# Which bank and which step two of a pair's projection thirds take, in a two-layer decoder step on one Trainium2 core

## The reference, cut to what matters

```python
q, z, gl, gate = b_project(xp, c_prompt, b_norm_g[j], b_w_ada[j], b_b_ada[j], b_w_in[j])
o_cmp, o_sel, o_win = nsa_prompt(q, comp_p[:, :, 0], comp_p[:, :, 1], gather_p, win_p, rel_bias_table)
...
ob = jnp.stack([o_cmp, o_sel, o_win], axis=2).reshape(n, t, N_BRANCH, N_HEADS, HEAD_DIM)
mix = jnp.sum(jax.nn.sigmoid(gl)[..., None] * ob * jax.nn.silu(z), axis=2)
```

## Time and profile before

| what | value |
|---|---|
| median of 3 runs | 1786.0 us (1785.25 to 1787.79) |
| the profiled execution | 1782.46 us, its span 1780.7 us |
| PE busy | 1623.2 us, 91% of the span |
| DVE, ACT, POOL busy | 911.3, 599.7, 501.1 us |
| mean granted clock of PE | 0.950 |

### The profile page before, as it was taken

One profiled execution on the slowest core, in us unless ns is written; L12 is line 12 of the kernel. 1 busy time (PEld: TensorE's weight loads), 2 busy tenths in 40 slices (PEclk: granted clock), 3 DMA queues, 4 the chain that ended last, 5 costly groups with the idle time before them and its releaser, 6 DMA issues.

```text
span 1780.7 us, 31773 instructions
## 1 busy us (share of the span) xinstructions
PE 1623.2 (91%) x11976; PEld 1453.3 (82%) x11976; DVE 911.3 (51%) x2356; ACT 599.7 (34%) x1315; POOL 501.1 (28%) x304
## 2 busy tenths in 40 slices
PE   3899999997896988799999999999999999998887
PEld 1688888886795987788888889888898888976777
DVE  1445455455325143455655556556555565577355
ACT  2523333343004042224434344343443434443112
POOL 0131322116531234281111111111102111049462
PEclk9899999999898988899999999999999999999998
DMA  9123232223321144310111131111110111133822
GB/s 351 50 99 125 92 111 101 101 102 132 119 95 72 54 165 126 86 36 22 39 37 34 31 77 40 60 34 28 34 40 13 34 28 34 28 98 110 270 72 107
DMA packets 81586, 146.20 MB, mean 82 GB/s; under 512 B 19059, under 2 KB 52883, under 8 KB 81267
## 3 DMA queue, kind: packets, MB, share of 16 engines
q1 hardware_dynamic: 68202, 129.69, 22.5%
q10 hardware_dynamic: 10288, 8.46, 1.5%
q0 software_dynamic: 2944, 6.04, 1.2%
HBM read 130.01 MB, written 19.35 MB: 84 GB/s over the span
## 4 chain that ended last, share of the span: by engine, by line
PE 81%; DVE 7%; ACT 4%; issue 3%; DMA 3%; SPq 1%; POOL 0%; ACTq 0%; DVEq 0%
PE PS L935 15%; PE PS L937 14%; PE PS L936 14%; PE PS L1182 9%; PE PS L1195 9%; PE PS L1162 4%; PE PS L1163 4%; PE PS L1274 2%; PE PS L1172 1%; PE PS L1191 1%; PE PS L1127 1%; PE PS L966 1%; ACT XT L1383 1%; ACT HT_r L1386 1%; DMA KD<-w_bo 1%
## 5 line engine op out<-in xcount | busy, mean ns | idle before, releaser
L935 PE MATMUL PS<-HT_r,WR_r 128*128 128x344 f32 x1368 | 461.7, 337 | 29.2 <-DVE XT_r L1650 24.4
L937 PE MATMUL PS<-HT_r,WR_r 128*128 128x344 f32 x1368 | 445.0, 325 | 0.0
L936 PE MATMUL PS<-XT_r,WR_r 128*128 128x344 f32 x1368 | 444.7, 325 | 0.0
L625 POOL TENSOR_TENSOR WR_r<-WR,ONE 128x1024 fp32r<-128x1024 f32 x65 | 125.8, 1936 | 1093.4 <-DMA WR<-w_b 645.6
L1462 ACT ACTIVATE PB<-PB,NM 128x257 f32<-128x257 f32 (+9 forms) x384 | 248.9, 650 | 176.2 <-DVE NM L1841 176.0
L935 PEld LDWEIGHTS PS<-HT_r,WR_r 128*128 128x128 f32 x1368 | 265.7, 194 | 34.7 <-issue 26.5
L936 PEld LDWEIGHTS PS<-XT_r,WR_r 128*128 128x128 f32 x1368 | 265.2, 194 | 0.0
L937 PEld LDWEIGHTS PS<-HT_r,WR_r 128*128 128x128 f32 x1368 | 264.3, 193 | 0.0
L1182 PE MATMUL PS<-CST,PB 128*128 128x128 f32 (+1 forms) x1360 | 227.0, 286 | 1.8 <-ACT PB L1458 1.5
L1854 DVE COPY PT<-PS 128x256 f32<-128x256 f32 (+2 forms) x192 | 121.6, 633 | 198.7 <-PE PS L1182 198.1
L1195 PE MATMUL PS<-PT,VT 128*64 128x128 f32 x2592 | 202.9, 284 | 5.2 <-DVE SS L1894 1.8
(11 more groups left out here) (289 smaller groups left out, 2342.8 us busy)
## 6 DMA issues: line engine op xcount, KB each, us to landing
WR<-w_ada SPq DMA_DIRECT2D x64, 512.0 KB, 5.1
WR<-w_b SPq DMA_DIRECT2D x32, 512.0 KB, 3.4
WR<-w_a SPq DMA_DIRECT2D x17, 512.0 KB, 5.6
STR<-scratch SPq DMA_DIRECT2D x128, 48.0 KB, 1.9
KD<-w_bo SPq DMA_DIRECT2D x9, 512.0 KB, 3.5
XT<-x SPq DMA_DIRECT2D x8, 516.0 KB, 15.1
HT<-x SPq DMA_DIRECT2D x8, 516.0 KB, 4.6
x_mid<-HT SPq DMA_DIRECT2D x8, 516.0 KB, 6.2
```

What stands on the lines that cost most here:

```text
L625: pool.tensor_tensor(high_r, raw, ONE[:, 0:1].unsqueeze(2).to_broadcast([P, NC, P]), ALU.mult).then_inc(sem("w_split"), 1)
L935: pe.matmul(out, hw[:, k, :], high, start=(k == 0), stop=False)
L936: pe.matmul(out, hw[:, k, :], low, start=False, stop=False)
L937: return pe.matmul(out, lw[:, k, :], high, start=False, stop=(k == NC - 1))
```

## The change

The table `spans` is written anew, two of the twelve thirds of a pair go through bank 3, and PE waits for the later of these two before it writes scores into that bank again:

```diff
@@ phase_plan
-            spans = [[(0, 1)], [(1, 1)], [(2, 1)], [(3, 1)], [(4, 1)], [(5, 1), (6, 1)],
-                     [(7, 1), (8, 1)], [(9, 1)], [(10, 1)], [(11, 1)], [(12, 1), (13, 1)], [(14, 3), (15, 3), (16, 2)]]
+            spans = [[(0, 1)], [(0, 1)], [(1, 1)], [(2, 1)], [(3, 1)], [(4, 1), (5, 1)],
+                     [(6, 1), (7, 1)], [(8, 1)], [(9, 1), (10, 1)], [(11, 1)], [(12, 1), (13, 1)], [(14, 3), (15, 3), (16, 2)]]
@@ number_fills
             elif ph == "b":
-                fl["bank"] = 7
+                fl["bank"] = 3 if (i - len(pl["prologue"])) % 12 in (1, 3) else 7
@@ pairs, on PE, ahead of the scores of a unit
+                            if b == "sel" and un["qb"] == 4 and s == 1:
+                                own_fills = pl["fills"][len(pl["prologue"]) + 12 * it:]
+                                pe.wait_ge(*evicted([fl for fl in own_fills[0:12] if fl["bank"] == 3][-1]))
```

## The result

| | before | after |
|---|---|---|
| median, same series (4 runs each) | 1786.89 us (1785.25 to 1789.07) | 1740.63 us (1737.70 to 1743.49) |
| ratio, 95% interval | | 0.9747 (0.9731 to 0.9764) |
| the profiled execution, its span | 1782.46, 1780.7 us | 1743.49, 1741.8 us |
| mean granted clock of PE | 0.950 | 0.960 |

The kernel is 46.3 us faster by the medians; the forecast was 42.3. In a later series five more runs of the changed kernel gave 1735.38 us in the median (1733.51 to 1744.28), against 1785.02 before.

A forecast was written before the change was run, and what follows sets the result against it. PE, busy for 91% of the span, loses time to step 0's wait for DVE and the lowered clock after it. 25.4 + 21.3 - (1.2 + 1.4 + 1.5 + 0.3) = 42.3 us off 1786.0 gives 1743.7 us; range 1737 to 1765.

The forecast's parts named there:

- The likeliest case: Whole kernel: the second third fills step 0's wait and the clock stays up; 1743.7 us, chance 0.81.
- Idle time of step 0: Step 0 of all eight pairs: a second third of 3.76 us covers PE's wait for DVE; gain 25.4 us less remainders.
- The clock: Between the L1172 groups of steps 0 and 1: clock stays up; 2.89 + 6 x 3.07 = 21.3 us gained.
- What remains: Steps 0 and 1: ACT's late copy 1.2 us, wait left at L1172 1.4, pair 0's tighter step and query weights 1.5.
- Steps 4, 9 and 10 at nothing: These steps each give up half a third (1.88 us); cost taken as 0, with 7.4 us kept for the range.
- The rival that moved the bubble there: Steps 4, 9 and 10: bare chain from scores to exponentials, waits plus clock 104 us lost, 1848 us; chance 0.04.
- Edits at no cost: Second bank of head 1, PE's new wait before selected block 4's scores, SP and POOL order: nothing; late copy would cost 0.43 us.
- the last about 1.5 us: Last pair: sign expected in the changed kernel's profile, this pair shorter by about 1.5 us, the others some 6 us each.
- up to 1.2 us off the last stage, or nothing: Last pair: page loads start one step earlier relative to its end, gaining up to 1.2 us; nothing was taken.
- The rival in which the clock still falls: Step 0: short waits that add up lower the clock, only idle time is gained, 21.0 us; 1765 us, chance 0.10.
- The rival in which the wait moves along: Step 0: a DVE step ahead of L1873 waits for the second third; no gain, 1786 us, chance 0.05.

The follow-up runs named there:

- the bank alone: Changed kernel's new bank and PE wait kept, thirds (24 matmuls each) back in the steps of the kernel before; 1784.39 us, ratio 1.0002 to the kernel before.
- the last pair as before: Changed kernel, but the last pair's three thirds (24 matmuls each) stand in steps 0, 1 and 2 again; 1739.41 us, ratio 0.9741 to the kernel before.
- POOL moved: Kernel before, thirds unmoved; POOL's query-weight split waits for the second scores after step 0; 1757.67 us, ratio 0.9852.
- the two kernels with late pages: Changed kernel with the last pair's selected pages loaded a step later, or its last third in step 2 and two in step 0; 1736.85 and 1739.54 us.
- the quarters: Changed kernel with POOL's split of the second layer's attention output in four instructions of 256 columns, not one of 1024; 1738.28 us, ratio 0.9745 to the kernel before.

## Why the prediction was right, and where it was off

The likeliest case came, within the range and 3 us below the forecast. That the total came so near is in part luck: the seven pairs gained 4.3 us more than their terms said, and the tail differs by 6.9 us between two executions of the changed kernel.

1. *Idle time of step 0*, 25.4 us less what remains. The mechanism holds: PE's order brings the gain, and the bank alone gives none. The seven pairs gained 23.1 us of idle time, where the terms give 19.8 (25.4 - 1.66 for the last pair - 1.05 - 1.4 - 1.5). Of the 3.3 us between them 1.3 lie outside the stretches of the earlier trace rows: half of the 1.26 us at L1182 in pair 0, and short waits at L1195. The other 2.0 are item 3.

2. *The clock*, 21.3 us. All eight stretches read 1.00, with 6.42 to 6.84 us between the two groups. PE is busy for 22.4 us less in the seven pairs, 3.2 us per pair. That lies between the row's 3.07 us and the 3.4 us by the Trainium skill's rule ("TensorE: Matmul & The Clock Gate", Terms); the trace shows somewhat less than the rule gives, here as in the tail (5.1 us of PE's time for 13.8 us at the lower level). What I had wrong is the certainty: I took the wait of 1.66 us that kept its clock as a case that always does. With the bank alone, and with the last pair as before, the same 1.66 us in the last pair read 0.91, and with POOL moved 1.66 us (once 1.73) read 0.91 twice and 1.00 five times. The change kept the clock in every profile with a wait of 0.7 us or less, and 1.66 us did not keep it every time.

3. *What remains*, 1.2 + 1.4 + 1.5. Too much by 2.0 us over the seven pairs, in which PE now stands idle for 1.9 us: ACT's late copy costs 0.15 to 0.24 us in three of them (0.6 where 1.05 was set), pairs 1 to 6 keep 0.25 and 0.30 us in two of them (0.55 where 1.4 was set), and pair 0 waits 0.67 us where 1.5 was set; its query weights, wanted a step earlier, were never late. The seven pairs were to gain 41.1 us by the prediction's own terms (19.8 and 21.3). With 3.3 us more of idle time and 1.1 us more of clock that is the 45.4 measured, within rounding.

4. *Steps 4, 9 and 10 at nothing*. Right: the 1.9 us of idle time that are left in the seven pairs all lie at the groups of L1176 and L1186 in steps 0 and 1, so half a third covers these steps. The rival that moved the bubble there fell.

5. *Edits at no cost*, and the last pair. Right for the bank and for PE's wait. The last pair did not bear out: "the last about 1.5 us" shorter was not seen, in one execution its tail is 4.8 us longer than before and in the other 2.1 us shorter, and the two kernels with late pages show no gain from the covered wait. The page loads, set at "up to 1.2 us off the last stage, or nothing", did move something. POOL's splits, which follow the loads, begin 46.5 instead of 51.5 us into the tail, and there the first of them holds up a DVE product of 0.29 us for 2.45, for which PE waits 1.8 us at L1199:

```profile
1554.89 2.45 DVE L1734 TENSOR_TENSOR STR<-STR,CST 128x128 f32<-128x128 f32 x1
...
1555.28 1.91 POOL L637 TENSOR_TENSOR XT_r<-MT,ONE 128x1024 fp32r<-128x1024 f32 x1
```

What that costs at the end is not shown; by the sums above it is 1.0 to 1.5 us or nothing. It adds a wait at which the clock fell in one of the two executions profiled.

The rival in which the clock still falls did not come in step 0. By the Trainium skill ("TensorE: Matmul & The Clock Gate", section "A second HAM failure mode: psum-queue depth-cycling") brief idling while banks are cycled makes the clock swing; in the changed kernel the clock falls after short waits only in the last pair, where no thirds are left to fill them (0.62 and 0.53 above), and there PE waits for DVE's copy; that the cycling of banks has a part in it no run shows. The rival in which the wait moves along fell with the wait itself: in step 0, 1.2 of 24.3 us are left.

## What to carry to other kernels

When PE waits for a chain on another engine, move independent matmuls into the gap before shortening the chain, and count the clock with the wait: here a wait of 3.5 us cost 3.1 us more behind it. Fill the gap whole: in one series half the fill brought 28.9 us and a quarter 12.1 us of the 49.6 that the whole brought, and in step 0 of these profiles only waits of up to 1.4 us left the clock up every time. Before crediting or blaming an edit for a few us, compare two executions of one program: here their tails differ by 6.9 us, 5.1 of it PE's own time at another clock.

## What the hardware showed that I had not expected

Some DVE operations that meet one of POOL's end only when POOL's does, however small they are. In the first execution of the changed kernel a DVE product of 14 columns, 0.30 us in the kernel before, started with POOL's subtraction and took as long:

```profile
1584.19 2.35 POOL L639 TENSOR_TENSOR MT_r<-MT,XT_r 128x1024 fp32r<-128x1024 f32 x1
1584.19 2.38 DVE L1794 SCALAR_TENSOR_TENSOR WR<-WR,CST 128x14 f32<-128x14 f32 x1
```

Others are not held: the copy of L1858 and the reduction of L1845, which read PSUM, take their usual time beside POOL, as does L1821 in pair 4 above, which started with POOL's L627. The product of L1898, for which PE then waits 3.7 us, comes behind the held one in DVE's order. The Trainium skill ("SBUF — State Buffer", Terms) says that the two engines share a pair of ports that is locked for a full instruction, and that the loser blocks and does not share. The trace agrees with the blocking. With the quarters DVE once did not get in between four POOL instructions that follow each other closely (2.85 us beside four of 2.32 us in all) and once did (0.65 us beside four of 2.37). When a DVE operation comes relative to POOL's thus changes its time, and an edit that moves POOL by a few us, as this one did in the last pair, shifts which of them are hit.
